# A squared-ReLU MLP's up projection in seven block products, with weight sums by adding DMAs and squares on GpSimd

## What is computed

```python
h = x + jnp.einsum('bte,ed->btd', mixed, w_o)
u = jax.nn.relu(jnp.einsum('btd,df->btf', rmsnorm(h, norm_ffn), w_up))
return h + jnp.einsum('btf,fd->btd', u * u, w_down)
```

## Time and profile before

| | |
|---|---|
| time, median of 3 executions | 3015.88 us (3015.17 to 3016.10) |
| span of the profiled execution, first to last instruction | 3009.8 us |
| busy: TensorE / VectorE / ScalarE / GpSimd | 2917.5 / 1630.4 / 987.6 / 327.6 us |
| DMA traffic | 327.29 MB, mean 109 GB/s |
| `merge_and_ffn`, from TensorE's first transposes to the end | 1321.6 to 3009.8 us |

### The profile page before, as it was taken

One profiled execution on the slowest core, in us unless ns is written; L12 is line 12 of the kernel. 1 busy time (PEld: TensorE's weight loads), 2 busy tenths in 40 slices (PEclk: granted clock), 3 DMA queues, 4 the chain that ended last, 5 costly groups with the idle time before them and its releaser, 6 DMA issues.

```text
span 3009.8 us, 45644 instructions
## 1 busy us (share of the span) xinstructions
PE 2917.5 (97%) x18136; PEld 2585.7 (86%) x18136; DVE 1630.4 (54%) x2259; ACT 987.6 (33%) x1826; POOL 327.6 (11%) x504
## 2 busy tenths in 40 slices
PE   7999899899999999879999999999999999999999
PEld 5788788788888999768999999889999997888887
DVE  5554354476566577844444544544445445455555
ACT  3331266455555333233222222222222222232221
POOL 2322200020001255620000000000000000000000
PEclk9999999999999999989999999999999999999999
DMA  7833332453223553513211211332111213333332
GB/s 257 257 130 123 107 90 71 126 159 112 73 86 91 174 153 111 184 68 112 70 57 57 82 59 71 133 104 72 56 57 59 82 70 110 118 126 126 126 133 98
DMA packets 285061, 327.29 MB, mean 109 GB/s; under 512 B 53644, under 2 KB 234478, under 8 KB 284850
## 3 DMA queue, kind: packets, MB, share of 16 engines
q1 hardware_dynamic: 284850, 324.38, 32.8%
HBM read 256.28 MB, written 67.78 MB: 108 GB/s over the span
## 4 chain that ended last, share of the span: by engine, by line
PE 54%; DVE 1%; ACT 0%; issue 0%; POOL 0%; POOLq 0%; ACTq 0%
PE mf_psO L2260 28%; PE mf_psT L2312 23%; PE mf_psO L2312 1%; PE mf_psO L2283 1%; PE mf_psT L2246 1%; PE mf_psO L2295 0%; ACT mf_whi L2040 0%; DVE mf_wlo L2119 0%; DVE mf_acc L2212 0%; DVE mf_acc L2222 0%; DVE mf_xlo L2131 0%; ACT mf_hs L2101 0%; DVE mf_acc L2141 0%; DVE mf_hs L2149 0%; ACT mf_xhi L2055 0%
## 5 line engine op out<-in xcount | busy, mean ns | idle before, releaser
L2212 DVE TENSOR_TENSOR mf_acc<-mf_psO,mf_acc 128x1024 f32<-128x1024 f32 x256 | 313.5, 1225 | 347.8 <-PE mf_psO L2260 346.7
L2312 PE MATMUL mf_psT<-mf_xhi,mf_wlo 128*128 128x384 f32 (+1 forms) x1440 | 459.7, 319 | 0.0
L2312 PE MATMUL mf_psT<-mf_xlo,mf_whi 128*128 128x384 f32 (+1 forms) x1440 | 459.6, 319 | 0.0
L2312 PE MATMUL mf_psT<-mf_xhi,mf_whi 128*128 128x384 f32 (+1 forms) x1440 | 459.4, 319 | 0.0
L2260 PE MATMUL mf_psO<-mf_whi,mf_uhi 128*128 128x512 f32 x1024 | 401.5, 392 | 4.0 <-DVE mf_acc L2212 2.2
L2260 PE MATMUL mf_psO<-mf_whi,mf_ulo 128*128 128x512 f32 x1024 | 399.3, 390 | 0.0
L2260 PE MATMUL mf_psO<-mf_wlo,mf_uhi 128*128 128x512 f32 x1024 | 399.2, 390 | 0.0
L2040 ACT ACTIVATE mf_whi<-mf_st 128x2048 fp32r<-128x2048 f32 x104 | 194.8, 1911 | 605.1 <-PE mf_psO L2260 603.2
L2312 PEld LDWEIGHTS mf_psT<-mf_xhi,mf_whi 128*128 128x128 f32 x1440 | 270.5, 188 | 1.6
L2312 PEld LDWEIGHTS mf_psT<-mf_xlo,mf_whi 128*128 128x128 f32 x1440 | 270.5, 188 | 1.6
L2312 PEld LDWEIGHTS mf_psT<-mf_xhi,mf_wlo 128*128 128x128 f32 x1440 | 270.5, 188 | 0.0
(11 more groups left out here) (209 smaller groups left out, 5536.8 us busy)
## 6 DMA issues: line engine op xcount, KB each, us to landing
mf_st<-in_w_up SPq DMA_DIRECT2D x48, 1024.0 KB, 6.4
mf_st<-in_w_down SPq DMA_DIRECT2D x48, 1024.0 KB, 4.9
wst<-in_w_in SPq DMA_DIRECT2D x24, 1024.0 KB, 5.3
pj_wst<-in_w_in SPq DMA_DIRECT2D x36, 512.0 KB, 6.1
scratch_proj<-pj_ob SPq DMA_DIRECT2D x48, 256.0 KB, 2.0
pj_xin<-in_x_prompt SPq DMA_DIRECT2D x16, 512.0 KB, 7.3
md_qn<-scratch_proj SPq DMA_DIRECT2D x64, 128.0 KB, 2.6
scratch_proj<-md_ob SPq DMA_DIRECT2D x64, 128.0 KB, 3.3
```

The costliest lines, as they stand in the source:

```text
L2212: nc.vector.tensor_tensor(acc[0:r, i, :], psO[k % 2][0:r, :], acc[0:r, i, :], ALU.add).then_inc(s["o_out"], 1)
L2312: last = nc.tensor.matmul(up_psum(t, f, b, cn), wa[b4][:, w0:w0 + P], xa[:, j, c0:c0 + cn], start=j == 0 and q == 0, stop=j == KD - 1 and ...
```

## The change

The up projection of a third is written as a 2x2 block product: `w_up` is cut at input 512 and at hidden column 2048, the rows of a third into an even and an odd half (384, 384 and 272 rows). Seven products of half the depth replace eight (Strassen's form with shared sums). For each of 16 steps p and each z of 1 to 7 there is one `up(t, p, z)` of 12 matmuls (4 slices, three each): 84 in a step where there were 96. The result of product 1 is copied out of PSUM (`snap`), and products 6, 5 and 3 go on adding into the same bank, with a copy after 6 and after 5; VectorE adds products 2, 7 and 4 to these copies (`add`). The four results, called 11, 22, 21 and 12, are the same four 128-wide slices-by-blocks that a step made before.

- Four sums of blocks of `w_up` (512x2048, 4.2 MB each) are made in DRAM: in `middle`, GpSimd issues four copies near the start and, at a third, a half and two thirds of the plan, four DMAs that add to their destination. A wait of GpSimd stands before the adds (`sum_begun`, `sum_added`) and one at the end of `middle`.
- Weights of the up projection are loaded in pieces of 128x512 (256 KB, rows of 512 bytes), 112 a third, into four staging buffers and a ring of seven hi/lo pairs (`split_u`); `w_down` is 1 MB a step as before, split in four parts (`split_d`).
- Sums of the normed rows' blocks are formed on chip once for each pair of tiles: `full_sum` (VectorE, 4), `hi_sum` (ScalarE, 4), `lo_sum` (VectorE, 4). The transposes of tile i-1 now stand after half of `out_proj(i)`.
- The relu is taken from SBUF (12: from PSUM), and its square, which was VectorE's L2187, is GpSimd's `square`.
- The first 14 products of a third (`LEADS`, steps 0 and 1) are interleaved by hand; after two of them stand the transposes of the last tile.
- In the last third the tile of new rows comes first. The residual x is loaded straight into `acc`.

```diff
+            def begin_sums():
+                for out, half in copied:
+                    nc.gpsimd.dma_start(out, half).then_inc(sum_begun, 16)
+            def add_halves():
+                pool.wait_ge(sum_begun, 64)
+                for out, half in added[0:2]:
+                    nc.gpsimd.dma_start(out, half, accum_op=ALU.add, max_dma_last_dim=8192).then_inc(sum_added, 16)
+            def add_third():
+                pool.wait_ge(sum_added, 32)
+                nc.gpsimd.dma_start(added[2][0], added[2][1], accum_op=ALU.add, max_dma_last_dim=8192).then_inc(sum_added, 16)
+            def add_fourth():
+                pool.wait_ge(sum_added, 48)
+                nc.gpsimd.dma_start(added[3][0], added[3][1], accum_op=ALU.add, max_dma_last_dim=8192).then_inc(sum_added, 16)
+            beside = {masks_at: make_masks, 8: begin_sums}
+            for k, do in enumerate((add_halves, add_third, add_fourth)):
+                beside[len(plan) * (2 + k) // 6] = do
+            run(Dn.gpsimd(pool), B.gpsimd(pool), A.gpsimd(pool), C.gpsimd(pool), beside)
+            pool.wait_ge(sum_added, 64)
...
+def half_sums(w_up, sums):
+    half, rows = DFF // 2, D // 2
+    top, low = slice(0, rows), slice(rows, D)
+    one, two = slice(0, half), slice(half, DFF)
+    first = [(sums[0], w_up[top, two]), (sums[1], w_up[top, one]), (sums[2], w_up[top, one]), (sums[3], w_up[low, one])]
+    added = [(sums[0], w_up[low, two]), (sums[2], w_up[top, two]), (sums[1], sums[0]), (sums[3], sums[1])]
+    return first, added
...
+        LEADS = [(0, 1), (0, 2), (1, 1), (1, 2), (0, 6), (1, 6), (0, 7), (0, 5), (0, 4), (0, 3), (1, 7), (1, 5), (1, 4), (1, 3)]
+        UPS = (1, 2, 6, 7, 5, 4, 3)
...
+        def chunk_src(p, z):
+            half = slice(0, D // 2), slice(D // 2, D)
+            f = DFF // 2
+            w = {1: w_up[half[0], 0:f], 2: w_up[half[1], 0:f], 4: w_up[half[1], f:2 * f],
+                 5: sums[0], 6: sums[1], 7: sums[2], 3: sums[3]}[z]
+            return w[:, p * P:(p + 1) * P].rearrange("(k p) n -> p k n", p=P)
...
+            def square(t, p, c):
+                n, v, rl = c_no(t, p, c), v_at(t, p, c), relu_at(t, p, c)
+                pool.wait_ge(s["relu_ready"], n + 1)
+                if c == 12:
+                    pool.wait_ge(s["ulo_ready"], n if p < 2 else n - 2)
...
+            def snap(t, p, z):
+                act.wait_ge(s["up_done"], up_no(t, p, {1: 1, 2: 6, 4: 5}[z]) + 1)
+                if p == 0 and z == 2:
+                    act.wait_ge(s["tlo_ready"], 4 * (group(t, NTS[t] - 1) + 1))
+                elif p == 1 and z == 4:
+                    act.wait_ge(s["ulo_ready"], c_no(t, 0, 22) + 1)
+                elif p >= 2 and z == 1:
+                    act.wait_ge(s["ulo_ready"], c_no(t, p, 11))
+                nc.scalar.activation(kept_at(t, p, z), bank(t, p, 1), ACT.Copy).then_inc(s["snap"], 1)
+            def relu(t, p, c):
+                n = c_no(t, p, c)
+                if c == 12:
+                    act.wait_ge(s["up_done"], up_no(t, p, 3) + 1)
+                else:
+                    act.wait_ge(s["v_ready"], v_no(t, p, c) + 1)
+                if n >= 2:
+                    act.wait_ge(s["sq_ready"], n - 1)
+                src = bank(t, p, 1) if c == 12 else v_at(t, p, c)
+                nc.scalar.activation(relu_at(t, p, c), src, ACT.Relu, scale=1.0 if c in (11, 22) else -1.0
+                                     ).then_inc(s["relu_ready"], 1)
+                act.wait_ge(s["relu_ready"], n + 1)
...
+                if c == 21:
+                    dve.wait_ge(s["snap"], s_no(t, p, 2) + 1)
...
+                    nc.vector.tensor_tensor(v_at(t, p, c), bank(t, p, 7), v_at(t, p, c), ALU.add).then_inc(s["v_begun"], 1)
+                    dve.wait_ge(s["v_begun"], NP * t + p + 1)
+                    dve.wait_ge(s["up_done"], up_no(t, p, 4) + 1)
+                    nc.vector.tensor_tensor(v_at(t, p, c), v_at(t, p, c), bank(t, p, 4), ALU.subtract
+                                            ).then_inc(s["v_ready"], 1)
+                    return
...
+            def lo_u(t, p, c):
+                n, v = c_no(t, p, c), v_at(t, p, c)
...
+                                          ).then_inc(s["usq_ready"], 1)
+                dve.wait_ge(s["uhi_ready"], n + 1)
+                nc.vector.tensor_tensor(u[:, u_slot(p, c), 1, u_cols(t, c)], v,
+                                        u[:, u_slot(p, c), 0, u_cols(t, c)].bitcast(F32), ALU.subtract
+                                        ).then_inc(s["ulo_ready"], 1)
...
+                for slot in range(3):
+                    full_sum(t, nt - 1, slot)
+                lo_sum(t, nt - 1, 4)
+                full_sum(t, nt - 1, 3)
+                for j in (5, 2, 6):
+                    lo_sum(t, nt - 1, j)
+                lo_normed(t, nt - 1)
+                lo_u(t, 0, 11)
+                add(t, 1, 11)
+                lo_u(t, 1, 11)
+                split_u(t, 7)
+                split_u(t, 8)
+                for j in range(4):
+                    split_d(t, 0, j)
+                split_u(t, 9)
+                add(t, 0, 22)
+                split_u(t, 10)
+                lo_u(t, 0, 22)
+                add(t, 0, 21)
+                lo_u(t, 0, 21)
+                split_u(t, 11)
+                lo_u(t, 0, 12)
+                split_u(t, 12)
+                split_u(t, 13)
+                add(t, 1, 22)
+                lo_u(t, 1, 22)
+                add(t, 1, 21)
+                lo_u(t, 1, 21)
+                lo_u(t, 1, 12)
+                split_u(t, 14)
+                for pos in range(nt - 1):
+                    add_down(t, 0, pos)
+                    for q in (range(15, 17), range(17, 19), range(19, 20), range(20, 21))[pos] if pos < 4 else ():
+                        split_u(t, q)
+                for p in range(2, NP):
+                    after = range(7 * p + 7, 7 * p + 14) if p + 1 < NP else range(0)
+                    add_down(t, p - 2, nt - 1)
+                    for j in range(4):
+                        split_d(t, p - 1, j)
+                    add(t, p, 11)
+                    lo_u(t, p, 11)
+                    for pos in after[0:4]:
+                        split_u(t, pos)
+                    add(t, p, 22)
+                    add(t, p, 21)
+                    lo_u(t, p, 22)
+                    lo_u(t, p, 21)
+                    add_down(t, p - 1, 0)
+                    lo_u(t, p, 12)
+                    if p + 1 < NP:
+                        for pos in range(1, nt - 1):
+                            for q in after[3 + pos:4 + pos]:
+                                split_u(t, q)
+                            add_down(t, p - 1, pos)
...
+                    if at == 1:
+                        if t == 0 and i == 0:
+                            turn(0, 2, False)
+                            turn(0, 3, False)
+                        if i:
+                            turn(t, i - 1, True)
...
+            def up(t, p, z):
+                c = up_no(t, p, z)
...
+                if p < 2:
+                    if z == 1 and p == 0:
+                        pe.wait_ge(s["lo_ready"], t_index(t, nt - 2, True) + 1)
+                        pe.wait_ge(s["o_out"], o_index(t, nt - 2, -1) + 1)
+                    if z == 1:
+                        pe.wait_ge(s["squared"], n0[t] + nt - 1 + p)
+                    if p == 0 and z in (6, 7, 5, 4):
+                        pe.wait_ge(s["tlo_ready"], 4 * g + (6, 7, 5, 4).index(z) + 1)
+                    if z == 7:
+                        pe.wait_ge(s["tf_ready"], 4 * g + 4)
+                    if z == 7 and p == 1 or z == 3 and p == 0:
+                        pe.wait_ge(s["lo_ready"], t_index(t, nt - 1, True) + 1)
+                elif z == 1:
+                    pe.wait_ge(s["relu_ready"], c_no(t, p, 11))
+                if z in (6, 5, 3):
+                    pe.wait_ge(s["snap"], s_no(t, p, {6: 1, 5: 2, 3: 4}[z]) + 1)
+                out = bank(t, p, 1 if z in (6, 5, 3) else z)
+                again = z in (6, 5, 3)
+                b, (wh, wl) = FACTOR[z], uw[c % NRING]
+                for kk in range(KH):
+                    for q, (wa, xa) in enumerate(((wh, xhb(b)), (wh, xlb(b)), (wl, xhb(b)))):
+                        last = nc.tensor.matmul(out, wa[:, kk, :], xa[:, kk, 0:HB[t]],
+                                                start=not again and kk == 0 and q == 0,
+                                                stop=kk == KH - 1 and q == 2, skip_group_check=again)
+                last.then_inc(s["up_done"], 1)
...
-                def up(f, b):
-                    c0, cn = bl[b]
-                    b4, k, i = wbuf("u", f // FP), up_index(t, f, b), up_pos[f, b]
...
-                        pe.wait_ge(s["sq_ready"], k - 3)
-                    for j in range(KD):
-                        w0 = j * FP * P + (f % FP) * P
-                        for q, (wa, xa) in enumerate(((whi, xhi), (whi, xlo), (wlo, xhi))):
```

(25 more changed lines are left out.)

1093 lines of the change are left out of this document (647 added, 446 removed).

## The result

The changed kernel takes **3057.82 us** (median of 4 executions, 3055.18 to 3061.55), where the kernel before, on the same chip, took 3015.53: a ratio of 1.0143, 95% interval 1.0129 to 1.0158. It is 42 us slower; 70 us faster was forecast, with 6% on slower.

The account below looks back on a forecast made before the run. TensorE, busy 2917.5 of 3009.8 us, was taken as the bound. Terms A to E, -90.8 + 18.3 + 4.7 - 10.5 + 8 = -70.3 us, gave a span of 2939.5 and a time of 2946 us; 8-in-10 range 2922 to 2985.

Parts of the forecast that it names:

- Term E: Weight sums in `middle`: copies and adds on DMA cost +8 us, bounds 0 and +40.
- a term that the forecast had put at nothing: TensorE's granted clock: new waits are each shorter than the 8.6 us idle seen at 0.98, so nothing added.
- issuing is hidden: In `middle`: the four copies are issued near 332 us, where GpSimd waits 22.8 us for something else anyway.
- Rival 1: In `middle`, sums and x loads collide on DMA: about +30 instead of +8, 2976 us; chance 12%.
- rival 3: In `middle`, GpSimd waits for the adds and `middle` for GpSimd: 166 us standing, 3104 us; chance 6%.
- Term A: Up projection in `merge_and_ffn`: 192 fewer matmuls in each third, other engines keep up, -90.8 us.
- the forecast's own sign: Prediction wrong outright if steady steps are not 2.1 us (1.5 in the last third) shorter than before.
- Terms B, C and D: `merge_and_ffn`: waits in each third's first 14 products +18.3 us, waits around the leads +4.7, earlier idle time gone -10.5.
- B: First 14 products of a third: TensorE waits 4.7, 4.7 and 8.9 us, mainly on VectorE's queue; +18.3 us.
- Rival 2: `merge_and_ffn`'s last third: VectorE and GpSimd block each other over the squares, 19 us more, 2965 us; chance 8%.
- Rival 4: Steady steps: saved matmuls return as waits between products sharing a bank, 48 x 1.5 us = 72, 3018 us; chance 2%.
- The 6.1 us between span and time: Whole kernel: median time 3015.88 us lies 6.1 us above the profiled span 3009.8, added to the forecast span.

## Why the prediction was wrong

- **Term E failed**: "+8 us", "bounds: 0 and +40". It measured +104 alone (109.9 us of span in the changed kernel: 93.8 of idle TensorE and 16.1 of slower matmuls at the lower clock, a term that the forecast had put at nothing). The first fault is "issuing is hidden": the copies' issue was costed, and their 16.8 MB never were. They took 36 us of TensorE at 330-400 us, where the attention's first loads stand in line, with no price in the sum at all. The second is the bound: it was the adds' own duration, over tasks with slack, while packet-for-packet service of 8 KB against 0.5 to 2 KB holds back *every* small transfer of SP's for as long as a big one lasts, so the loads for k, v and q, the gains' stores and the recurrence's loads were each late once, by 15 to 28 us beyond their slack.
- **Rival 1** named this mechanism ("sums and loads collide"); its price of +30 was a third of what it costs, so that it still ended faster than before. The only slower case was rival 3, by another path. The rule of the Trainium skill that I had cited, that all DMAs interleave, spoke for rival 1. I weighed it against DMA shares of 0.31 to 0.35, which are windows of `merge_and_ffn`, where no sum runs: in `middle` the mean was 0.39, and 0.42 at 330-400 us. And no share shows the grain of the interleaving, 8 KB against 512 bytes.
- **Rival 3**, the one that ended slower, did not happen: at 900.40 and 1092.72 us GpSimd issued its adds without a wait. That the result is slower is no merit of it.
- **Term A right, but for the pace**: -90.8 forecast. TensorE's busy time in the stage went from 1669.2 to 1599.8 us, -69.4. The difference of 21 is the 512-column pace, 48 steps at 0.44 or 0.27 us and 17 output projections at 0.22. "Down projection ... keeps its count" was right, and its price changed all the same: I took a duration over to a kernel with another SBUF map. By the forecast's own sign it was wrong outright here too: steady steps are 1.7 us (1.3 in the last third) shorter, not 2.1 (1.5), though the up products alone are 2.10 and 1.54 shorter.
- **Terms B, C and D** together: forecast +12.5 of idle time, measured +3.1 (stage's idle time 19.0 us before, 22.1 after). In the windows from the last output projection to the first down projection TensorE stood 2.7, 2.7 and 6.2 us, where B said 4.7, 4.7 and 8.9. The square on GpSimd took 833 ns, not 1.07 us, and B has two of them in its longest chain. The waits were the ones named (`mf_uw4l` 4.8 us, the turn 4.1).
- **Rival 2 fell**: splits on VectorE took 686 ns and low parts 555 with GpSimd's squares in the same steps, and 686 and 558 without. No row shows the exclusive lock of the Trainium skill (SBUF — State Buffer, "SBUF: two separate sides"), but nothing put it to the test either. In the step from 1600 us the squares run at 1600.87, 1607.46, 1609.09 and 1610.47 us, for 0.83 us each, and no split or low part of VectorE's runs beside one for more than 0.04 us. **Rival 4 fell** too: TensorE was busy 298.00 of 298 us in the last third's steps.
- Two errors of the stage partly cancelled (the pace, 22 us too little; idle time, 9 too much). Without the sums the kernel took 2949.5 us, where the forecast without term E is 2938; beside the 2946 it would have looked like a hit, by luck.
- The 6.1 us between span and time were too many as well: the profiled execution of the changed kernel took 3055.18 us with a span of 3053.4, so 1.8 lie around the instructions. The rest was the execution that happened to be profiled, and it changes no verdict.

## What to carry to other kernels

Cost every DMA that a change adds by what it does to the others in flight: a bulk transfer on a second queue takes one packet for each of the first's, so the first goes at the pace of the bulk's packets, 8 KB long here, and small loads that something waits for are late for its whole length. Cut bulk transfers to some 256 KB, keep two in flight at most, and put them where the loads ahead have slack; the same sums cost 104 us whole and some 16 so. Smaller packets alone are no way out: they held GpSimd at its own next DMA. And when a change moves buffers, take no matmul's pace over from before: look at how the operands' addresses lie to each other.
